# Expert weights in 8 KB runs with permuted rows, and an item's two result halves summed by GpSimd

## The reference, cut to what matters

```
def moe_ffn(h, ...):                       # h: 320 x 1024
    g_prob = softmax(h @ w_rg + b_rg)      # 4 groups, the best one is taken
    e_logits = (h @ w_re + b_re)           # 32 experts, those of the chosen group
    ... top 2 of the group's 8 experts, gate = g_p * e_p / sum(e_p)
    for each expert e, its tokens t:
        a, u = split(h[t] @ w_e_in[e], 2)              # w_e_in[e]: 1024 x 1024
        y = (silu(a) * u) @ w_e_out[e]                 # w_e_out[e]: 512 x 1024
        out[t] += y * gate
```

## Time and profile before

| | |
|---|---|
| time, median of 3 runs | 1299.65 us (1297.51 to 1302.85) |
| profiled execution | 1297.03 us, its span 1295.2 us |
| busy share of the span | PE 85%, DVE 69%, ACT 49%, POOL 21% |
| HBM read, written | 299.97 MB, 14.73 MB |
| expert weight loads | 192 of 1 MB (128 + 64) |
| `w_hi` copies in the expert items, L973 | 157, 1903 ns each |
| `w_lo` differences in the expert items, L1566 | 157, 2318 ns each |
| `y_low` copies, L986 | 32, 1024 ns each |

### The profile page before, as it was taken

How to read it: one execution, slowest core, us unless ns; L and a number is a source line. 1 busy time by engine, 2 the same in 40 slices (tenths; PEclk the granted TensorE clock), 3 DMA queues, 4 the chain that set the end, 5 groups by cost and what they waited for, 6 DMA issues and landing times.

```text
span 1295.2 us, 13399 instructions
## 1 busy us (share of the span) xinstructions
PE 1104.2 (85%) x4460; PEld 761.4 (59%) x4460; DVE 894.2 (69%) x974; ACT 634.2 (49%) x639; POOL 267.6 (21%) x227
## 2 busy tenths in 40 slices
PE   5798899888899999999854799999999999999960
PEld 2365568566687666678644556666666666666640
DVE  3868843367464333345596699999999999999957
ACT  3654232222322222332221477777777777777732
POOL 0331940010001000000460741111111111111210
PEclk8798989988999555589785699999999999999985
DMA  9767243153725500024623589999999999999933
GB/s 321 253 238 257 94 152 130 48 169 104 272 73 137 205 0 0 0 98 162 213 68 109 190 336 389 389 393 393 395 395 393 397 391 396 394 390 400 397 110 116
DMA packets 102661, 303.33 MB, mean 234 GB/s; under 512 B 10740, under 2 KB 10788, under 8 KB 102118
## 3 DMA queue, kind: packets, MB, share of 16 engines
q1 hardware_dynamic: 92888, 282.75, 58.6%
q0 software_dynamic: 9744, 20.19, 5.2%
HBM read 299.97 MB, written 14.73 MB: 243 GB/s over the span
## 4 chain that ended last, share of the span: by engine, by line
PE 59%; DVE 18%; DMA 7%; ACT 7%; issue 5%; POOL 4%; SPq 0%; ACTq 0%; POOLq 0%; DVEq 0%
PE banks L1968 9%; PE banks L1976 7%; PE banks L1964 7%; PE banks L1694 6%; PE banks L1700 6%; DVE w_lo L1566 6%; ACT w_hi L973 5%; PE banks L1696 4%; DMA w_raw<-in_w_in 3%; DVE w_lo L1061 3%; PE banks L1727 2%; PE banks L1957 2%; ACT w_hi L816 2%; PE banks L1983 1%; DMA w_raw<-in_w_ada 1%
## 5 line engine op out<-in xcount | busy, mean ns | idle before, releaser
L1566 DVE TENSOR_TENSOR w_lo<-w_raw,w_hi 128x2048 fp32r<-128x2048 f32 x157 | 361.3, 2318 | 36.8 <-ACT w_hi L973 36.8
L973 ACT ACTIVATE w_hi<-w_raw 128x2048 fp32r<-128x2048 f32 x157 | 295.5, 1903 | 0.2 <-issue 0.2
L1061 DVE TENSOR_TENSOR w_lo<-w_raw,w_hi 128x2048 fp32r<-128x2048 f32 x72 | 173.2, 2423 | 137.8 <-ACT w_hi L816 137.7
L816 ACT ACTIVATE w_hi<-w_raw 128x2048 fp32r<-128x2048 f32 x72 | 136.5, 1910 | 210.5 <-PE banks L1700 94.7
L1968 PE MATMUL banks<-w_lo,xT_item 128*128 128x512 f32 x512 | 150.5, 416 | 45.2 <-DVE w_lo L1566 45.2
L1964 PE MATMUL banks<-w_hi,xT_item 128*128 128x512 f32 x512 | 158.9, 433 | 4.2 <-ACT w_hi L973 2.8
L1694 PE MATMUL banks<-w_hi,h_hi 128*128 128x512 f32 x384 | 142.2, 411 | 13.1 <-ACT w_hi L816 12.6
L1968 PEld LDWEIGHTS banks<-w_lo,xT_item 128*128 128x128 f32 x512 | 93.5, 193 | 91.3 <-DVE w_lo L1566 73.1
L1964 PEld LDWEIGHTS banks<-w_hi,xT_item 128*128 128x128 f32 x512 | 96.0, 193 | 39.1 <-issue 14.3
L1976 PE MATMUL banks<-w_raw,hiddenT 128*128 128x512 f32 x248 | 111.4, 592 | 0.0
L1700 PE MATMUL banks<-w_lo,h_hi 128*128 128x512 f32 x384 | 108.2, 404 | 2.4 <-DVE w_lo L1061 2.4
(11 more groups left out here) (438 smaller groups left out, 1579.3 us busy)
## 6 DMA issues: line engine op xcount, KB each, us to landing
w_raw<-in_w_e_in SPq DMA_DIRECT2D x128, 1024.0 KB, 7.3
w_raw<-in_w_e_out SPq DMA_DIRECT2D x64, 1024.0 KB, 6.0
w_raw<-in_w_in SPq DMA_DIRECT2D x32, 1024.0 KB, 9.0
w_raw<-in_w_ada SPq DMA_DIRECT2D x24, 1024.0 KB, 7.2
bias_rows<-in_b_in SPq DMA_DIRECT2D x16, 256.0 KB, 4.8
w_raw<-in_w_ret_proj SPq DMA_DIRECT2D x4, 1024.0 KB, 17.2
w_raw<-in_w_fox_proj SPq DMA_DIRECT2D x4, 1024.0 KB, 18.8
w_raw<-in_w_o SPq DMA_DIRECT2D x4, 1024.0 KB, 5.1
```

What stands on the lines that cost most here:

```text
L816: nc.scalar.activation(whi[n % NSPL][:], raw[n % NRAW][:], ACT.Copy).then_inc(hi_done, 1)
L973: nc.scalar.activation(whi[ss][:], raw[j][:], ACT.Copy).then_inc(hi_done, 1)
L1061: V.tensor_tensor(wlo[n % NSPL][:], raw[n % NRAW][:], whi[n % NSPL][:].bitcast(F32), ALU.subtract).then_inc(lo_done, 1)
L1566: V.tensor_tensor(wlo[ss][:], raw[j][:], whi[ss][:].bitcast(F32), ALU.subtract).then_inc(lo_done, 1)
```

## The change

The rows of the expert matrices are dealt out so that a partition's rows lie next to each other in DRAM: partition p holds rows 8p to 8p+7 of `w_e_in` (4p to 4p+3 of `w_e_out`), and a load of two of them is one run of 8 KB. The activations are brought into the same order: DVE writes `h2` with its columns permuted (reading at steps of 8 floats, for which the product goes through the buffer `affine_tmp`), the router's weights are loaded with the same rows, and `hidden` is written permuted (reading at steps of 4 floats).

ACT copies both halves of `y` out of PSUM (`y_halves`, a new buffer `y_high`), and POOL adds them in SBUF (`sum_item`), ahead of its scatter. DVE's `y_sum` stays for the last item alone. PE's wait for free `y` banks is now for ACT's copies.

```diff
+    yHi = at("y_high", [SLOTS, 2, 512], F32, 55296)
-    w_in_e = i["w_e_in"][0].rearrange("e (k p) n -> e p k n", p=P)
-    w_out_e = i["w_e_out"][0].rearrange("e (k p) n -> e p k n", p=P)
+    w_in_e = i["w_e_in"][0].rearrange("e (p k) n -> e p k n", p=P)
+    w_out_e = i["w_e_out"][0].rearrange("e (p k) n -> e p k n", p=P)
...
-        pool.dma_start(wr[:, :, 0:NG], i["w_rg"][0].rearrange("(k p) n -> p k n", p=P)).then_inc(wr_in, 16)
+        pool.dma_start(wr[:, :, 0:NG], i["w_rg"][0].rearrange("(p k) n -> p k n", p=P)).then_inc(wr_in, 16)
...
+        def sum_item(e):
+            pool.wait_ge(y_lo, e + 1)
+            nc.gpsimd.tensor_tensor(ySb[:], yHi[:], yLo[:], ALU.add).then_inc(y_drained, 1)
...
-        def store_item(e):
+        def store_item(e, summed=True):
             pool.wait_ge(y_written, 16 * e)
             nc.gpsimd.tensor_copy(row1[:], row[:, bass.ds(e, 1)]).then_inc(row_cp, 1)
             pool.wait_ge(row_cp, e + 3 - STATIC)
+            if summed:
+                sum_item(e)
             pool.wait_ge(y_drained, e + 1)
...
         gather_item(3)
+        sum_item(0)
         scatter_item(0)
         for e in range(3, STATIC):
             gather_item(e + 1)
+            pool.wait_ge(y_written, 16 * (e - 2))
+            sum_item(e - 2)
             scatter_item(e - 2)
...
-        def y_low(e, end_sub):
+        def y_halves(e, end_sub, first):
+            act.wait_ge(used, end_sub + 1)
+            if not first:
+                act.wait_ge(y_drained, e)
+            nc.scalar.activation(yLo[:], banks[SLOTS:P, 2:4, :], ACT.Copy)
+            nc.scalar.activation(yHi[:], banks[0:SLOTS, 2:4, :], ACT.Copy).then_inc(y_lo, 1)
+        def y_low(end_sub):
...
             if second:
-                y_low(e - 2, sub(e - 1, 5))
+                y_halves(e - 2, sub(e - 1, 5), first)
...
-            st(V.tensor_tensor(ht, xt, m2[0:rows, 1, :], ALU.mult))
+            st(V.tensor_tensor(g1x[0:rows, :], xt, m2[0:rows, 1, :], ALU.mult))
             st.settle()
-            st(V.tensor_tensor(ht, ht, m2[0:rows, 0, :], ALU.add), h2_ready)
+            st(V.tensor_tensor(ht.rearrange("r (k p) -> r k p", k=KD), g1x[0:rows, :].rearrange("r (p k) -> r k p", k=KD),
+                               m2[0:rows, 0, :].rearrange("r (p k) -> r k p", k=KD), ALU.add), h2_ready)
...
         def hidden(e):
             dve.wait_ge(silu_ok, e + 1)
-            V.tensor_tensor(hid[:], aA[:], auS[:, 1, :], ALU.mult).then_inc(hid_ok, 1)
+            V.tensor_tensor(hid[:].rearrange("s (k p) -> s k p", k=4), aA[:].rearrange("s (p k) -> s k p", k=4),
+                            auS[:, 1, :].rearrange("s (p k) -> s k p", k=4), ALU.mult).then_inc(hid_ok, 1)
...
             hidden(e - 1)
             item_lo(e, 1)
-            if second:
-                y_sum(e - 2, third)
             item_lo(e, 2)
...
         item_lo(n_items, 1)
-        y_sum(n_items - 2, True)
         hidden_low(n_items - 1)
-        y_sum(n_items - 1, True)
+        y_sum(n_items - 1)
...
             if second:
-                pe.wait_ge(y_drained, e - 1)
+                pe.wait_ge(y_lo, e - 1)
             pe.wait_ge(hh_split, e)
```

More of the change, by code:

```diff
@@ L718, in _ @@
         pool.wait_ge(evacuated, CI["wo0"] + 1)
-        pool.dma_start(wr[:, :, 0:NG], i["w_rg"][0].rearrange("(k p) n -> p k n", p=P)).then_inc(wr_in, 16)
-        pool.dma_start(wr[:, :, NG:], i["w_re"][0].rearrange("(k p) n -> p k n", p=P)).then_inc(wr_in, 16)
+        pool.dma_start(wr[:, :, 0:NG], i["w_rg"][0].rearrange("(p k) n -> p k n", p=P)).then_inc(wr_in, 16)
+        pool.dma_start(wr[:, :, NG:], i["w_re"][0].rearrange("(p k) n -> p k n", p=P)).then_inc(wr_in, 16)
         pool.dma_start(br[:, 0:NG], bcast(i["b_rg"][0], P)).then_inc(wr_in, 16)
@@ L801, in _ @@
         store_item(n_items - 2)
-        store_item(n_items - 1)
+        store_item(n_items - 1, False)
     TS = [("ret", 0), ("fox", 1), ("mix", 2)]
@@ L1000, in _, with item @@
         x_high(1)
-        def item(e, second):
+        def item(e, second, first=False):
             item_hi(e, 0)
@@ L1015, in _ @@
         item(1, False)
+        item(2, True, True)
         act.wait_ge(nit_ready, 1)
         n_items = NE + act.value_load(nit[0:1, 0:1], min_val=0, max_val=EXTRA - 1)
-        with act.Fori(2, n_items) as e:
+        with act.Fori(3, n_items) as e:
             item(e, True)
@@ L1022, in _ @@
         item_hi(n_items, 1)
-        y_low(n_items - 2, sub(n_items - 1, 5))
+        y_halves(n_items - 2, sub(n_items - 1, 5), False)
         hidden_high(n_items - 1)
         act.wait_ge(y_drained, n_items - 1)
-        y_low(n_items - 1, sub(n_items, 1))
+        y_low(sub(n_items, 1))
         def first_gate(t):
@@ L1584, in hidden_low, with y_sum @@
                             hdT[:, :, 0:SLOTS].bitcast(F32), ALU.subtract).then_inc(hh_split, 1)
-        def y_sum(e, written):
-            if written:
-                dve.wait_ge(y_written, e * 16)
+        def y_sum(e):
+            dve.wait_ge(y_written, e * 16)
             dve.wait_ge(y_lo, e + 1)
@@ L1595, in _, with item_steps @@
         x_low(1)
-        def item_steps(e, second, third):
+        def item_steps(e):
             item_lo(e, 0)
@@ L1608, in item_steps @@
             x_low(e + 1)
-        item_steps(1, False, False)
-        item_steps(2, True, False)
+        item_steps(1)
         n_items = NE + dve.value_load(nit[0:1, 0:1], min_val=0, max_val=EXTRA - 1)
-        with dve.Fori(3, n_items) as e:
-            item_steps(e, True, True)
+        with dve.Fori(2, n_items) as e:
+            item_steps(e)
         item_lo(n_items, 0)
@@ L2013, in _ @@
         hidden_T(n_items - 1)
-        pe.wait_ge(y_drained, n_items - 1)
+        pe.wait_ge(y_lo, n_items - 1)
         pe.wait_ge(hh_split, n_items)
```

## The result

| | before | after |
|---|---|---|
| time, median (range) in the same comparison | 1301.25 us (1297.51 to 1305.01) | 1321.79 us (1320.26 to 1326.4) |
| ratio | | 1.0167, 95% interval 1.0141 to 1.0193 |
| profiled execution, its span | 1297.03, 1295.2 us | 1320.26, 1318.4 us |
| period of an item, 780 to 1222 us | 16.37 to 16.39 us, 26 of them | 17.16 to 17.19 us, 24 of 25; one of 18.05 |

The change makes the kernel slower by 1.7%. 1324 was forecast, and an item 0.81 us longer; it is 0.79. The periods in this document are the distances between neighbouring `y_low` copies on ACT.

A forecast was written before the change was run, and what follows sets the result against it. Bound: the expert loop's quarter j=3 waiting on ACT behind PE's hidden transpose, not loads. 30 x (0.47 + 0.34) = 24.3, h2 +1.4, end -0.6 gave +25.1 us, a median of 1324 us; range 1303 to 1342.

The forecast's parts named there:

- What bounds the kernel: Expert loop: a cycle through PE's hidden transpose, ACT and DVE sets the 16.38 us item; loads are ahead.
- the named wait: ACT's `hidden_high`, ahead of quarter j=3's copy, waits for PE's transpose, 1.4 us in each of 27 items.
- `y_sum` leaves DVE: Expert item, before j=2: removing its 1.21 us from DVE gains nothing, since j=3 waits for ACT and PE.
- The second copy on ACT: Expert item on ACT: the added copy takes 0.92 us, hidden in a 1.44 us wait for PE.
- The turns: GpSimd's sum and DVE's `w_lo` alternate whole: sum 2.25 us after j=1, j=2's `w_lo` ends 2.17 after the sum.
- The term of 0.47: Delay in us of j=3's `w_lo` per item from the GpSimd sum, without the longer hidden product.
- The read at steps, h = 0.34: DVE's hidden product, reading at steps of four floats, takes 0.34 us longer per item; bounds 0 to 0.68.
- With 0.34 DVE's j=1 is done at 1017.93; PE needs it at 1018.07, so nothing else moves.: Expert item: the longer hidden product still lets j=1's `w_lo` finish before PE needs it, so no further delay.
- h2: DVE's multiply-adds before the router read at steps of eight floats: +1.4 us in total, between 0 and 2.7.
- The ends: Last item's chain: `y_sum(30)` leaves DVE ahead of `hidden_low`, -0.9 us, or -0.6 with the longer hidden product.
- What would show it: Expected trace signs: GpSimd sum 2.3 to 2.6 us, longer `w_lo` at j=2, item 17.2, PE's j=3 wait +0.8.
- The sum: Whole kernel: 24.3 us over 30 items, +1.4 for h2, -0.6 at the end, +25.1 us in all.

The follow-up runs named there:

- e5: Kernel before with ACT's `w_hi` copy of j=3 moved ahead of `hidden_high` and DVE's `w_lo` of j=3 ahead of `hidden_low`; 1299.81 us, ratio 1.0002.
- e12: Kernel before with the 8 KB runs alone, hidden columns permuted where ACT and DVE read PSUM, h2 still at steps; 1302.47 us, ratio 1.0016.
- e3: Changed kernel with GpSimd adding only the first 512 of the 1024 columns; 1302.48 us, ratio 1.0046.
- e1: Kernel before with the 8 KB runs and all permutations, the sum left on DVE; 1305.57 us, ratio 1.0061.
- e2: Changed kernel without the 8 KB runs and permutations, the sum on GpSimd; 1314.52 us, ratio 1.0131.
- e4: Changed kernel with `hidden` read and written in order again; 1317.28 us, ratio 1.0155.
- e11: e5's order plus 8 KB runs, sum on DVE, hidden columns permuted where ACT and DVE read PSUM; against the kernel before 1289.4 us, ratio 0.9923.
- e9: Kernel before with 8 KB runs, the permutation made by PE's transposes loading blocks at steps; 1334.86 us, ratio 1.0293.
- e8: e5 with 8 KB runs, the permutation made by PE's transposes loading blocks at steps; 1291.48 us, ratio 0.994 against the kernel before.

## Why the prediction was right

- *What bounds the kernel.* Right. e5 takes the named wait out and the item shrinks to 15.38, until the loads bind; e12 changes the loads and nothing moves.
- *`y_sum` leaves DVE, worth nothing.* Right: e3 has it off DVE, and its item is the 16.60 of e1, which has it on. (e3's time is 3 us less than e1's; that lies ahead of the items and behind them.)
- *The second copy on ACT, 0.92 in the cover of a 1.44 wait.* The cover held (0.64 is left), but the copy was 1.05: `y_high` starts 1.04 after `y_low` and `w_hi` 0.93 after that. It cost nothing because `w_lo` of j=2 was ready at 1015.55, a microsecond before the sum ended.
- *The turns.* 2.25 and 2.17 were read from before's rows at 641 and 740 us; measured 2.24 and 2.16. The term of 0.47 is 0.48 in e2. The Trainium skill (SBUF — State Buffer, section "Who interferes with whom") says that a DVE instruction with two inputs in SBUF contends with a GpSimd instruction that reads SBUF, through a read interface that they share, and the trace agrees. That `au_sum`, with one input in PSUM, took 1.21 beside a GpSimd addition agrees as well. But that the two alternate, instruction by instruction, is no rule: before's trace has GpSimd waiting through two `w_lo` in a row (732.26, above). In an item the turn came as forecast, with 1.23 us behind `w_lo` of j=1 in which DVE had nothing ready.
- *The read at steps, h = 0.34.* Measured 0.39 on DVE (1071 against 676 ns), 0.77 ns an element against the 0.66 taken from a reduction. On the cycle it came to 0.31 beside the sum (17.17 less e4's 16.86): the sum follows `w_lo` of j=1 after 2.24, in e2 after 2.32, and 0.08 is lost there.
- *"With 0.34 DVE's j=1 is done at 1017.93; PE needs it at 1018.07, so nothing else moves."* Wrong by a little. In e1 h costs 0.22 an item with no sum in the way. PE's product of j=1 follows the one before it after 1.06 instead of 0.93 and takes 1.21 instead of 1.10, its weight loads no longer overlap what runs before, and the transpose behind it is later by 0.23 in all. The chain's 1018.07 is not the first use: before's timeline has PE load the first weights of that product at 1017.68, 0.09 after the end of `w_lo`:

```profile
1017.68 0.89 PEld L1968 LDWEIGHTS banks<-w_lo,xT_item 128*128 128x128 f32 x4
```

- *h2.* Its stepped additions took 1.99 to 2.06 against 1.22, 0.77 to 0.84 more each. The stretch from the first of these operations to the slot table grew by 1.55; 1.4 was taken.
- *The ends.* The step that was off: −0.6 was forecast and the tail (from the end of the last item's plain product to the span's end) is 2.3 shorter. The mechanism was there: from the last plain product to PE's next one it is 0.75 shorter. But PE's last four groups of products took 2.07, 1.59, 1.09 and 1.09 where before they took 2.07, 1.91, 1.91 and 1.21, 1.2 us less in all. The granted clock was 0.50 from 1247.3 to 1254.1 before, and from 1272.9 to 1276.3 after; PE had waited 3.23 and 2.10 ahead of it. That the shorter wait is why the full clock came back sooner is not shown, and this part was luck.
- *What would show it.* The two kinds of `w_lo`, the hidden product and the item were as said, and GpSimd's rows were 2.69 where 2.3 to 2.6 was said. One sign was not: I said that PE's wait at j=3 grows by 0.8. It fell from 1.07 to 0.40, and the wait ahead of j=2 grew from 0.29 to 1.53. PE loses the time one quarter earlier, because its own product of j=2 stands behind the held-back `w_lo`.
- *The sum.* 25.1 forecast, 23.2 between the two spans (20.5 between the medians): about 24.2 over the items (0.9 of it in the one item of 18.05), 1.3 ahead of them and −2.3 behind. That the 1.3 is so near the 1.4 for h2 is luck. This execution came to the first of the h2 operations 1.45 sooner (670.40 against 671.85), h2 took 1.55 of that back, and another 1.2 came with the loop's start: there GpSimd's part in the gather takes 6.07 where before it takes 2.85, and the first two `y_low` lie 20.4 apart instead of 16.4.
- *Two slips that change nothing.* The earlier trace rows has 412 GB/s twice and no 413, and 1299.65 + 25.1 is 1324.75.

## What to carry to other kernels

Before work is moved to GpSimd, list which DVE instructions beside it have two inputs in SBUF: each pair goes one after the other, so what counts is not GpSimd's time but how much of it sticks out of DVE's gaps, here 2.24 us into a gap of 1.2. Where DVE leaves no gap, GpSimd may wait much longer, here 10.7 us. An engine that looks full is relieved in vain as long as its instruction order makes it wait for another; take that wait away first, and read in the chain which resource is next in line before a second change is priced. In these runs a permutation was paid where single words are read from or written to SBUF, on DVE and in PE's weight loads alike, and was free where ACT and DVE empty PSUM.

## What the runs showed of the hardware that was not expected

- Under four `w_lo`, with `y_sum` and `hidden_low` between them, GpSimd got no turn for 10.7 us (e11's addition: 12.97, done 2.23 after DVE's last `w_lo`), and its gather waits in the same way (e5: 11.52 instead of 0.95). At 740 us, though, GpSimd went between two `w_lo` in a row (8.11 for the pair). What decides who goes next was not found.
- PE's weight load of a 64x128 block at steps of four floats is dearer by 0.1 us (e9, five records: 0.88 against 0.48 us), as a DVE read is.
- ACT and DVE read PSUM at steps of four floats at no cost (1024 and 1208 ns for 64x1024, in order 1024 and 1217).
- PE's granted clock fell to 0.55 to 0.59 over some 4 us in single items after a wait of 1.44 to 1.55 us (in e9 of 1.1, in e12 twice of 1.05, in e8 once of 0.6), and the item was 0.8 to 2.1 us longer, while the same wait in the items around left it at 1.00.
